# Reordering the end of the routing stage of a hybrid encoder layer with 32 experts

## What is computed

```python
g_prob = jax.nn.softmax((xt @ w_rg + b_rg).astype(jnp.float32), axis=-1)
g_top, g_idx = lax.top_k(g_prob, 1)
...
e_top, e_loc = lax.top_k(e_in, TOP_K)                       # TOP_K = 2, within the group
weight = g_top * jax.nn.softmax(e_top, axis=-1)
eid = (g_idx * EXPERTS_PER_GROUP + e_loc).reshape(-1)
order = jnp.argsort(eid)
xs = xt[tok_s]
a = jax.nn.silu(lax.ragged_dot(xs, w_gate, sizes)) * lax.ragged_dot(xs, w_up, sizes)
ys = lax.ragged_dot(a, w_down, sizes) * weight.reshape(-1)[order][:, None]
out = jnp.zeros_like(xt).at[tok_s].add(ys)
```

## Time and profile before

| | |
|---|---|
| median of three executions | 4223.26 us (4223.26, 4225.6, 4206.2) |
| the profiled execution | 4211.02 us |
| its span | 4209.0 us |
| PE busy | 4103.9 us, 98% of the span |
| PE weight loads | 3411.4 us, 81% |
| DVE | 2045.3 us, 49% |
| ACT | 1423.7 us, 34% |
| POOL | 740.6 us, 18% |
| DMA | 840.53 MB, mean 200 GB/s |

### The profile page before, as it was taken

One profiled execution on the slowest core, in us unless ns is written; L12 is line 12 of the kernel. 1 busy time (PEld: TensorE's weight loads), 2 busy tenths in 40 slices (PEclk: granted clock), 3 DMA queues, 4 the chain that ended last, 5 costly groups with the idle time before them and its releaser, 6 DMA issues. The chain is left out here.

```text
span 4209.0 us, 60644 instructions
## 1 busy us (share of the span) xinstructions
PE 4103.9 (98%) x20066; PEld 3411.4 (81%) x20067; DVE 2045.3 (49%) x3161; ACT 1423.7 (34%) x2510; POOL 740.6 (18%) x1020
## 2 busy tenths in 40 slices
PE   8999999999999999999999999599999999999997
PEld 7888888888888888888888888487888888888886
DVE  3554443443433433433433433577656566765664
ACT  2422311311311311311311311366555555655553
POOL 2000000001001000000000000234333333333333
PEclk9999999999999999999999999799999999999999
DMA  8786456455455455555555545577756466765562
GB/s 245 245 306 243 145 193 198 161 192 189 170 190 189 171 189 190 176 184 190 180 180 187 183 180 184 209 238 246 256 172 237 164 234 214 255 212 191 197 217 85
DMA packets 278468, 840.53 MB, mean 200 GB/s; under 512 B 47952, under 2 KB 99408, under 8 KB 226688
## 3 DMA queue, kind: packets, MB, share of 16 engines
q1 hardware_dynamic: 228400, 716.61, 50.0%
q0 software_dynamic: 49936, 121.90, 8.6%
HBM read 717.60 MB, written 178.45 MB: 213 GB/s over the span
## 5 line engine op out<-in xcount | busy, mean ns | idle before, releaser
L1095 PE MATMUL bank<-hT_hi,w_slot 128*128 128x512 f32 x2176 | 862.5, 396 | 8.7 <-DVE w_slot L883 7.2
L1097 PE MATMUL bank<-hT_hi,w_slot 128*128 128x512 f32 x2176 | 849.0, 390 | 0.0
L1096 PE MATMUL bank<-hT_lo,w_slot 128*128 128x512 f32 x2176 | 848.5, 390 | 0.0
L1727 PE MATMUL e_bank<-e_w_hi,e_xT_hi 128*128 128x512 f32 x1312 | 521.9, 398 | 14.2 <-DVE e_xT_lo L1653 12.2
L1729 PE MATMUL e_bank<-e_w_hi,e_xT_lo 128*128 128x512 f32 x1312 | 514.2, 392 | 0.0
L1728 PE MATMUL e_bank<-e_w_lo,e_xT_hi 128*128 128x512 f32 x1312 | 513.2, 391 | 0.0
L1658 DVE TENSOR_TENSOR e_w_lo<-e_raw,e_w_hi 128x1024 fp32r<-128x1024 f32 x384 | 443.9, 1218 | 115.4 <-ACT e_w_hi L1609 115.4
L1095 PEld LDWEIGHTS bank<-hT_hi,w_slot 128*128 128x128 f32 x2176 | 409.1, 188 | 106.6 <-issue 25.0
L1097 PEld LDWEIGHTS bank<-hT_hi,w_slot 128*128 128x128 f32 x2176 | 409.1, 188 | 87.3
L1096 PEld LDWEIGHTS bank<-hT_lo,w_slot 128*128 128x128 f32 x2176 | 409.6, 188 | 81.4
L1609 ACT ACTIVATE e_w_hi<-e_raw 128x1024 fp32r<-128x1024 f32 x376 | 366.2, 1053 | 0.0
(11 more groups left out here) (325 smaller groups left out, 6674.8 us busy)
## 6 DMA issues: line engine op xcount, KB each, us to landing
w_slot<-split_weights SPq DMA_DIRECT2D x353, 1024.0 KB, 4.8
e_raw<-in_w_exp_gate_dram SPq DMA_DIRECT2D x128, 512.0 KB
e_raw<-in_w_exp_up_dram SPq DMA_DIRECT2D x128, 512.0 KB
e_raw<-in_w_exp_down_dram SPq DMA_DIRECT2D x128, 512.0 KB
split_weights<-w_slot SPq DMA_DIRECT2D x50, 1024.0 KB, 5.7
h_rows<-h_rows SPq DMA_DIRECT2D x64, 512.0 KB, 7.6
x_rows<-in_x_dram SPq DMA_DIRECT2D x32, 512.0 KB, 5.4
raw<-in_w_in_dram SPq DMA_DIRECT2D x30, 512.0 KB, 6.9
```

What stands on the lines that cost most here:

```text
L1095: pe.matmul(out, hi, x_hi, start=first, stop=False)
L1096: pe.matmul(out, hi, x_lo, start=False, stop=False)
L1097: return pe.matmul(out, lo, x_hi, start=False, stop=last)
L1727: pe.matmul(out_p, hi, x_hi, start=first, stop=False)
```

## The change

Six edits; what is computed stays the same.

1. `route`, DVE: `weigh` moves from behind `place_rows` to ahead of the wait for PE's rank products.
2. `route`, DVE: the five writes of `bounds` move from ahead of `place_rows` to behind the one-hot rows. A new tile `start` holds first*128, so that `first` stays as it is for them.
3. `route`, ACT: four of the eight high parts of expert 0 are made ahead of `listed`, four behind it.
4. `route`, DVE: the low parts of the first two chunks (`done_early=2`) are made while DVE waits for `lists`.
5. `route`, POOL: the first gather of rows is issued here, once column 0 of `row_index` is written (`first_rows`); `experts` only waits for it.
6. `experts`, DVE: the low parts of gate chunks 2 and 3, then `evacuate(0)`, then the low parts of the four up chunks, then the memsets.

```diff
             @block.gpsimd
@@
                 po.wait_ge(got_in, 16)
+                x_at = weights["x_at"]
+                po.wait_ge(first_rows, 1)
+                po.tensor_copy(x_at[:, :], row_index[:, 2:3, 0]).then_inc(weights["x_at_set"], 1)
+                hold(po, weights["x_at_set"], 1)
+                po.indirect_dma_start(out=weights["rows"][:, :], out_offset=None, in_=h1[0:h1.shape[0] // 2, :],
+                                      in_offset=bass.IndirectOffsetOnAxis(ap=x_at[:, 0:1], axis=0))\
+                  .then_inc(weights["rows_in"], 16)
             @block.scalar
@@
+                def split_hi(chunks):
+                    for c in chunks:
+                        a.wait_ge(weights["raw_in"][c], 16)
+                        a.activation(weights["w_hi"][:, c, :], weights["raw"][:, c, :], ACT.Copy)\
+                         .then_inc(weights["hi_ready"], 1)
                 exponentials(a, r).then_inc(exp_ready, 1)
+                split_hi(range(weights["early"] // 2))
                 for j in range(2 * TILES):
...
-                for c in range(weights["early"]):
...
+                split_hi(range(weights["early"] // 2, weights["early"]))
             @block.vector
@@
+                v.wait_ge(exp_ready, 1)
+                weigh(v, link, r, tb)
                 v.wait_ge(counted, 1)
                 count_up_to(v, link, r, tb, ranks[:, TILES * E:2 * TILES * E], E)
@@
+                link(v.tensor_scalar(start[:, :], first[:, :], float(P), None, ALU.mult))
...
+                link(place_rows(v, link, r, tb, start))
...
+                for j in range(2 * TILES):
...
                 v.tensor_copy(bounds[:, 0, :], first[:, :])
                 v.tensor_copy(bounds[:, 1, :], upto[:, :])
...
-                v.wait_ge(exp_ready, 1)
-                weigh(v, link, r, tb)
...
+                for c in range(weights["done_early"]):
+                    v.wait_ge(weights["hi_ready"], c + 1)
+                    v.tensor_tensor(weights["w_lo"][:, c, :], weights["raw"][:, c, :],
+                                    weights["w_hi"][:, c, :].bitcast(FP32), ALU.subtract)\
+                     .then_inc(weights["lo_ready"], 1)
                 v.wait_ge(listed_up, 1)
@@
-                v.tensor_tensor(row_index[:, 2:, 0], code[:, :], second[:, :], ALU.subtract)
+                v.tensor_tensor(row_index[:, 2:, 0], code[:, :], second[:, :], ALU.subtract).then_inc(first_rows, 1)
@@ experts, gpsimd
-                gather_rows(0)
+                hold(po, rows_in, 16)
                 gather_base(-1)
@@ experts, vector
                 total = count_tiles(v)
+                for c in range(weights["done_early"], GC):
+                    split_lo(0, c)
+                evacuate(0)
+                for c in range(GC, 2 * GC):
+                    split_lo(0, c)
                 v.memset(aT_hi[:, :, :].bitcast(FP32), 0.0)
@@
-                for c in range(2 * GC):
-                    split_lo(0, c)
-                evacuate(0)
                 v.wait_ge(consts_in, 32)
```

More of the change, by code:

```diff
@@ L1299, in load_expert_chunk, with route @@
     sp.dma_start(dst, expert_chunk(t, e, c)).then_inc(weights["raw_in"][c], 16)
-def route(nc, t, tb, records, keep, weights):
+def route(nc, t, tb, records, h1, keep, weights):
     G, E = t["w_rg"].shape[1], t["w_re"].shape[1]
@@ L1323, in route @@
         upto, first, spare = sb("r_upto", [P, E]), sb("r_first", [P, E]), sb("r_spare", [P, E])
+        start = sb("r_start", [P, E])
         tile_row_f, tile_row = sb("r_tile_row_f", [P, 1]), sb("r_tile_row", [P, 1], I32)
@@ L1482, in experts @@
         raw, w_hi, w_lo = weights["raw"], weights["w_hi"], weights["w_lo"]
-        rows = sb("e_rows", [P, D])
+        rows, x_at = weights["rows"], weights["x_at"]
         xT_hi, xT_lo = sb("e_xT_hi", [P, KD, P], F32R), sb("e_xT_lo", [P, KD, P], F32R)
@@ L1504, in experts @@
         aT_ready, a_hi, a_ready = sem("e_aT_ready"), sem("e_a_hi"), sem("e_a_ready")
-        rows_in, x_at_set = sem("e_rows_in"), sem("e_x_at_set")
+        rows_in, x_at_set = weights["rows_in"], weights["x_at_set"]
         y_at_set, out_at_set = sem("e_y_at_set"), sem("e_out_at_set")
@@ L1805, in encoder_block @@
         chunks = 3 * F // P
-        weights = dict(chunks=chunks, early=2 * F // P, raw=sb("e_raw", [P, chunks, D]),
+        weights = dict(chunks=chunks, early=2 * F // P, done_early=2, raw=sb("e_raw", [P, chunks, D]),
                        w_hi=sb("e_w_hi", [P, chunks, D], F32R),
@@ L1809, in encoder_block @@
                        raw_in=[ctx.enter_context(nc.semaphore(f"e_raw_in{c}")) for c in range(chunks)],
+                       rows=sb("e_rows", [P, D]), x_at=sb("e_x_at", [P, 1], I32),
                        hi_ready=ctx.enter_context(nc.semaphore("e_hi_ready")),
+                       lo_ready=ctx.enter_context(nc.semaphore("e_lo_ready")),
+                       rows_in=ctx.enter_context(nc.semaphore("e_rows_in")),
+                       x_at_set=ctx.enter_context(nc.semaphore("e_x_at_set")),
                        consts_in=ctx.enter_context(nc.semaphore("e_consts_in")))
-        route(nc, t, tb, records, keep, weights)
+        route(nc, t, tb, records, h1, keep, weights)
         experts(nc, t, h1, out2, keep, weights, tb)
```

34 lines of the change are left out of this document (14 added, 20 removed).

## The result

| | before | with the change |
|---|---|---|
| median, 20 executions each | 4218.90 us (4204.95 to 4225.6) | 4229.32 us (4224.47 to 4237.6) |
| span of the profiled execution | 4209.0 us | 4230.3 us |
| start of routing (L95) to PE's first expert matmul | 41.53 us | 32.90 us |
| from there to the end | 1507.0 us | 1539.6 us |

The ratio is 1.0029 [1.0021, 1.0037], some 10 us slower, where I had forecast 10.9 us faster. The stretch that the change reorders did get shorter, by 8.6 us. The loop behind it, which I had taken as untouched, got 32.6 us longer in the profiled executions.

What follows compares the result with a forecast made beforehand. Bound: PE in the experts' loop, with a 42 us chain over other engines before it. Terms 1.64 + 5.37 + 3.9 = 10.9 us off 4217.1 gave 4206.2 us, a gain of 0.26%; range 4193 to 4222.

Steps and rivals of the forecast that it cites:

- Nothing in that loop is changed, so nothing is to be won in it: Experts' loop: PE busy 1471.5 of 1507 us, taken as unchanged behind its first expert matmul.
- what follows should move along: Behind PE's first expert matmul at 2702.00: everything moves by as much as that instruction does.
- Weights and bounds: `route`, DVE: one-hot rows start 1.64 us earlier, from 1.77 + 0.36 less an overhang of 0.49.
- Low parts in DVE's wait: `route`, DVE: two low parts of 1.15 us end at 2679.94, wanted at 2680.77; margin 0.8 us, cost nothing.
- High parts ahead of `listed`: `route`, ACT: four take 3.84 us, the fourth ending near 2670.5, 4 us before ACT is wanted; costs nothing.
- ACT being stuck: `route`: loads share bandwidth evenly, chunks land at 2683.2, PE starts 1.6 us later than before, 4218.7; chance 0.05.
- First gather in `route`: POOL: gather issued at 2683.17, landing 4.46 us later at 2687.63, 7.0 us earlier than before.
- The hand-over waits for the landing: Between blocks: POOL leaves only at 2687.63; gain 9.2, 4207.9 us; chance 0.22 together with a slower gather.
- A longer gather: First gather beside SP's reload: 7.9 against 4.4 us, 7.4 us gain remain, 4209.7; chance 0.22 shared with a late hand-over.
- Order on DVE: `experts`: second `xT_lo` no longer queues behind weights' low parts, PE starts at 2691.08; 3.9 us won.
- The clock: First expert matmuls: clock rises sooner because PE's pause shrinks from 5.4 to 1.5 us; gain 13.0, 4204.1; chance 0.05.
- nothing is kept: Loop: POOL's and the weights' chain hold PE, so the start's gain is given back, 4217.1 us; chance 0.08.

Runs made afterwards that it cites:

- e5_gap480: The change plus an unused 480-byte tile behind `x_at`, so all operands leave 320 to 512 bytes again; against the kernel before: 4215.4 us, 0.9996.
- e2_before_plus32: The kernel before plus one unused 32-byte tile per partition ahead of `xT_hi`, nothing else: 4229.5 us, ratio 1.0029 to before.
- e6_no_early_gather: The change without edit 5, first gather issued in `experts` and all tiles where they lay before: 4212.8 us, 0.9983 to the kernel before.
- e16_late_gather_outer_tiles: The change with 480 unused bytes, tiles and semaphores still outside, but the first gather issued in `experts`: 4209.6 us, 0.9988 to the kernel before.

## Why the prediction was wrong

**The step that failed** is in its first paragraph: "Nothing in that loop is changed, so nothing is to be won in it", and with it "what follows should move along". No instruction of the loop was changed, but its operands' addresses were, by a tile of 4 bytes, and the tail of its last block. The parts, taken from single traces and from pairs of kernels, add up to what was measured within its interval:

| part | us | from |
|---|---|---|
| head | -8.6 | 41.53 to 32.90 |
| operands 32 bytes apart | +13.9 | change against `e5_gap480`, medians (some 8 to 19 by the two intervals); `e2_before_plus32` gives +12.2 by its ratio |
| end of the program | +6.1 | 7.7 to 13.85 |
| sum | +11.4 | measured +12.2 (8.9 to 15.6) by the ratio |

Without the placement the change is worth nothing that can be told: `e5_gap480`'s 0.9996 is -1.7 us, against -2.3 from its head (33.16) and end. Without the early gather as well, -7.2 us (`e6_no_early_gather`) and -5.1 (`e16_late_gather_outer_tiles`) stand beside heads shorter by 4.9 and 5.6 us. These two beat both kernels, with intervals that just leave out 1.

The placement's 14 us are less than its matmuls lost. A tile of rows takes 17.72 us before and 18.10 with the change (median of start to start), 31 us over 82 tiles. With fast matmuls PE runs into its waits more: behind the first expert matmul 6.8 us for `xT_lo` before and 7.6 in `e5_gap480`, against 3.5 with the change. Summed over the loop, tiles start late (against the median distance of two tiles) by 25 to 43 us in the fourteen kernels at 227 ns and by 12 to 20 in the five slower ones. Between `e5_gap480` (33.0) and the change (20.1) that takes 13 of the 31 us back, and their loops differ by the rest, 18.5 us. The loops of the profiled executions spread: without the early gather 1507 to 1525 us at 227 ns against 1528 at 232 to 235, with it 1521 to 1530 against 1537 to 1540. The profiled execution of before had the shortest loop of all 19, which makes the 32.6 us of the table look like more than it is. That PE's pauses take back the rest is read from these traces; no run tests it alone.

Point by point:

- *Weights and bounds*: right in kind, 0.86 us instead of 1.64 (one-hot rows at 14.49, before 15.35). The overhang was 1.31 us, not 0.49. At 2664.39 one instruction of `weigh` on four numbers took 0.71 us, and 0.14 before, which is 0.57 of the 0.82 us by which the overhang was larger; it ended at 2665.10, and POOL's memset, which had begun at 2661.57, at 2665.08. In all ten kernels that have edit 1 it took 0.71 to 1.03 us and ended 7.25 us behind L95, where the memset ended at 7.22; in the other nine it runs behind the memset and took 0.14. I had laid the moved work into DVE's wait and left out what POOL did there. By the Trainium skill's page SBUF — State Buffer, section Who interferes with whom, the two share a port pair that one instruction locks to its end; the trace agrees for this one instruction, while the other DVE instructions beside the same memset kept their usual length.
- *Low parts in DVE's wait*: right. They end at 2678.08 and DVE still stood 0.96 us for `lists`.
- *High parts ahead of `listed`*: right, and so the rival of ACT being stuck fell. The chunks landed in turn, the fourth high part ended 10.8 us behind L95, with 4.03 us to spare. Without this edit 1.4 us are lost.
- *First gather in `route`*: issued 6.0 us earlier behind L95 (29.71 to 23.70), where the prediction had 7.0, and landed after 4.2 us, not 4.46: right in kind. The rule that I had set against it, a shared port that delays descriptors, didn't bite: the issue took 0.97 us, among DVE's writes.
- *The hand-over waits for the landing*: the rival happened. POOL's drain took 4.49 us, where 0.14 was usual, and DVE started at 2687.04, 4.5 us behind the end of the issue, not 1.36. I gave 9.2 us for this case, and 8.6 came; `weigh`'s term, 0.8 us short, is more than the rest.
- *A longer gather*: not in the change, since the wait in the hand-over keeps SP's reload away. It did come in the two kernels without the early gather (6.3 and 7.0 us).
- *Order on DVE*: the largest part, 7.0 us when undone. The edits depend on one another: undone one by one they cost 7.0, 1.4, 0.9 and, for the gather, 2.8 to 3.5 us, together 12 to 13 where the head is 8.6 shorter, and the gather alone brings nothing.
- *The clock*: the granted clock was at half (1.2 GHz) for the first expert matmuls again, from 2690.75 to about 2696.2, 5.5 us, against 4.0 before. So the rival that it would rise sooner did not come: PE had stood less, 1.77 us, and yet the half rate lasted longer. In the eight kernels with this pause of 1.77 us it lasted 3.1 to 5.6 us, so the pause doesn't set it.

```profile
2690.00:2694.00 4.00, 3.25 (x8) 2.58 (x9) 4.00 (x6) 1.28 (x1) 1.79 (x3) 0.50 0.97 357
2694.00:2698.00 4.00, 4.00 (x15) 3.16 (x14) 3.04 (x8) 0.00 (x0) 0.00 (x0) 0.72 1.01 377
```

- *Waits in the loop*: a reading of mine was wrong. The 12.2 us that I put into the loop, and that alone spoke for *nothing is kept*, hold the 5.39 us ahead of the first expert matmul, which belong to the head. The loop's own are 6.8 us.
- *The last sentence* held: I had named a stretch behind the first expert matmul that grows by over 5 us as what would prove me wrong. As a rival it stood only as "nothing is kept", the gain given back. That it could be made worse had no case, and my reading of the measurement's noise was too wide as well: with 20 executions a difference of 0.1% could be told.

## What to carry to other kernels

A change that makes a tile in another place moves the addresses of what is allocated behind it; list them before and after, and keep the distance between a matmul's two operands as it was; 480 unused bytes did that here. An edit's gain is read where the chain ends, and in these kernels a gather issued just ahead of the end of a block was waited for by the block. When a kernel that is one engine's for 98% loses time, compare that engine's instructions of the same shape first: here 5 to 8 ns of 227 were more than the whole loss.

## What the runs showed of the hardware

- A float32 matmul with a stationary operand of 128x128 and a moving one of 128x512 followed the last by 227 ns when the addresses of the two lay a multiple of 256 bytes apart (0, 256 and 512 more than before were tried), and by 231 to 235 ns when they lay 32, 64 or 96 bytes off that, at a granted clock of 1.00 in both. That is 2 to 3.5% of the interval, and 13.9 us of 4219. The Trainium skill's page SBUF — State Buffer, section Who interferes with whom, gives PE two read ports that are independent of each other; in these runs the interval depended on the distance between the two addresses, so here the measurement differs; which of the two reads waits no trace shows.
- The end of a block on POOL waited for an indirect DMA in flight: its drain took 4.49 to 4.72 us in six kernels, and 0.23 in the four in which POOL had waited for the landing itself.
- POOL's last drain took 9.1 to 9.3 us in all ten kernels whose first gather is issued in `route`, and 0.47 us in the nine others, with the last store's issue coming 2.65 us sooner in the ten. The cause is open.
